# Three modulation tiles moved from the first gate group into the last attention steps

## The reference, cut to what matters

```python
c_act = jax.nn.silu(c)
for l in range(2):
    mod = c_act @ w_ada[l] + b_ada[l]                 # 6 * 1024 values
    sh_m, sc_m, gt_m, sh_f, sc_f, gt_f = jnp.split(mod, 6, axis=-1)
    h = rms_norm(x, g_mix[l]) * (1.0 + sc_m) + sh_m
    z = h @ w_in[l] + b_in[l]                         # qa ka va qi ki wi qb kb vb ga gb
    ...                                               # index scores, top 128, two attentions
    merged = sigmoid(ga) * y_a + sigmoid(gb) * y_b    # y_a = att_a @ w_oa, y_b = att_b @ w_ob
    x = x + gt_m * (merged @ w_out[l])
    h2 = rms_norm(x, g_ffn[l]) * (1.0 + sc_f) + sh_f
    x = x + gt_f * ((silu(gate) * up) @ w_down[l])    # gate, up = split(h2 @ w_gu[l])
```

## Time and profile before

| | us |
|---|---|
| median of 3 runs | 3172.62 |
| lowest, highest | 3166.37, 3175.24 |
| the profiled execution | 3175.28 |
| its span in the profile | 3173.7 |
| VectorE's first and last modulation tile of layer 0 in the attention steps | 289.39, 358.22 |

### The profile page before, as it was taken

How to read it: one execution, slowest core, us unless ns; L and a number is a source line. 1 busy time by engine, 2 the same in 40 slices (tenths; PEclk the granted TensorE clock), 3 DMA queues, 4 the chain that set the end, 5 groups by cost and what they waited for, 6 DMA issues and landing times.

```text
span 3173.7 us, 36875 instructions
## 1 busy us (share of the span) xinstructions
PE 3027.0 (95%) x14098; PEld 2309.5 (73%) x14098; DVE 1705.9 (54%) x2840; ACT 1258.9 (40%) x1912; POOL 1097.6 (35%) x538
## 2 busy tenths in 40 slices
PE   6999999999989999999998999999999998999998
PEld 4666777888856667788886777877777886666664
DVE  5687673222257868422213454655677137666664
ACT  4355434223245553422324444323334234455543
POOL 1242344444423324354442554444444441000001
PEclk9999999999999999999998999999999998999999
DMA  5122563443321137374332333524442335799995
GB/s 228 53 61 73 173 200 113 142 130 100 117 80 54 60 100 241 124 308 144 95 115 81 107 120 113 193 85 117 136 128 67 93 106 223 299 385 384 383 380 208
DMA packets 188508, 501.29 MB, mean 158 GB/s; under 512 B 20080, under 2 KB 98032, under 8 KB 172224
## 3 DMA queue, kind: packets, MB, share of 16 engines
q1 hardware_dynamic: 165808, 417.24, 38.9%
q0 software_dynamic: 13200, 49.32, 4.1%
q10 hardware_dynamic: 9344, 32.61, 3.0%
HBM read 463.83 MB, written 35.29 MB: 157 GB/s over the span
## 4 chain that ended last, share of the span: by engine, by line
PE 77%; DVE 12%; ACT 4%; DMA 3%; issue 2%; ACTq 1%; POOL 1%; DVEq 0%; SPq 0%; POOLq 0%
PE banks L741 18%; PE banks L743 18%; PE banks L742 18%; PE banks L1483 5%; PE banks L1464 3%; PE banks L1466 2%; PE banks L1465 2%; DMA ring<-in_w_all 2%; PE banks L856 1%; PE banks L877 1%; PE banks L733 1%; PE banks L866 1%; DVE abuf L2377 1%; ACT w_hi L1568 1%; PE banks L837 1%
## 5 line engine op out<-in xcount | busy, mean ns | idle before, releaser
L3063 POOL TENSOR_TENSOR w_lo<-ring,w_hi 128x1024 fp32r<-128x1024 f32 (+1 forms) x375 | 908.2, 2424 | 1377.0 <-ACT w_hi L1568 1376.8
L742 PE MATMUL banks<-h_lo,w_hi 128*128 128x512 f32 x2104 | 827.4, 393 | 0.0
L741 PE MATMUL banks<-hx_hi,w_hi 128*128 128x512 f32 (+2 forms) x1400 | 592.4, 423 | 20.2 <-POOL w_lo L3063 9.1
L1568 ACT ACTIVATE w_hi<-ring 128x1024 fp32r<-128x1024 f32 (+1 forms) x375 | 388.8, 1038 | 551.4 <-DMA ring<-in_w_all 482.5
L743 PE MATMUL banks<-hx_hi,w_lo 128*128 128x512 f32 (+2 forms) x1400 | 553.9, 396 | 0.0
L742 PEld LDWEIGHTS banks<-h_lo,w_hi 128*128 128x128 f32 x2104 | 399.3, 190 | 88.6 <-issue 11.0
L741 PEld LDWEIGHTS banks<-hx_hi,w_hi 128*128 128x128 f32 (+2 forms) x1400 | 266.7, 191 | 133.3 <-issue 62.4
L743 PEld LDWEIGHTS banks<-hx_hi,w_lo 128*128 128x128 f32 (+2 forms) x1400 | 266.0, 190 | 61.0
L741 PE MATMUL banks<-hf_hi,w_hi 128*128 128x512 f32 x704 | 274.8, 390 | 0.1
L743 PE MATMUL banks<-hf_hi,w_lo 128*128 128x512 f32 x704 | 274.0, 389 | 0.0
L2547 DVE TENSOR_TENSOR arena<-sgs,banks 128x512 f32<-128x512 f32 x44 | 30.3, 689 | 327.7 <-PE banks L743 327.7
(11 more groups left out here) (450 smaller groups left out, 5267.5 us busy)
## 6 DMA issues: line engine op xcount, KB each, us to landing
ring<-in_w_all SPq DMA_DIRECT2D x352, 512.0 KB, 3.9
arena<-in_w_all SPq DMA_DIRECT2D x26, 2048.0 KB, 13.9
arena<-in_w_all SPq DMA_DIRECT2D x100, 512.0 KB, 4.7
ring<-in_w_all SPq DMA_DIRECT2D x46, 1024.0 KB, 7.3
arena<-in_w_all SPq DMA_DIRECT2D x25, 1024.0 KB, 9.3
x<-in_w_all SPq DMA_DIRECT2D x23, 1024.0 KB, 9.6
abuf<-in_w_all SPq DMA_DIRECT2D x32, 512.0 KB, 5.5
routed<-abuf POOLq DMA_DIRECT2D x1, 12288.0 KB, 50.9
```

The costliest lines, as they stand in the source:

```text
L741: pe.matmul(bank[0:m, :], upper, hi, start=first, stop=False)
L742: pe.matmul(bank[0:m, :], upper, lo, start=False, stop=False)
L1568: act.activation(hi_at(u)[:, 0:n], raw_at(u)[:, 0:n], ACT.Copy).then_inc(w_upper, 1)
L3063: pool.tensor_tensor(lo_at(u)[:, 0:n], raw_at(u)[:, 0:n], hi_at(u)[:, 0:n], ALU.subtract)\
```

## The change

`EARLY` becomes 11. The attention steps that take a tile are now a list, `BESIDE_STEPS`: 17, 19, 21, 23, 25 as before, and then every step from 26 to 31, where before it was 27, 29 and 31. Gate group 0 takes none, the groups 1 to 7 three each as before. The places of the tiles behind the early ones are counted from the first of them, so that they start with place 0. SyncE's list follows: 11 tiles through place 3, and no tile loads in gate group 0. The second block has its own number (`EARLY2`) and is unchanged.

```diff
-EARLY, EARLY2 = 8, 16
+EARLY, EARLY2 = 11, 16
+BESIDE_STEPS = (17, 19, 21, 23, 25, 26, 27, 28, 29, 30, 31)
...
-            buf = (3 if self.turn < early else self.turn % 4) if n == 2 else 2 + self.turn % 2
+            buf = (3 if self.turn < early else (self.turn - early) % 4) if n == 2 else 2 + self.turn % 2
...
                 for t in range(8):
                     load()
-                    if t < 7:
+                    if 0 < t < 7:
                         load_tile()
                         load_tile()
                     load()
-                    if t < 6:
+                    if 0 < t < 6:
                         load_tile()
...
-                    if s >= 17 and s % 2:
-                        modulate_beside(16 + (s - 17) // 2, v1)
+                    if s in BESIDE_STEPS:
+                        modulate_beside(16 + BESIDE_STEPS.index(s), v1)
...
-                    for k in range(16 + EARLY + 3 * t, 19 + EARLY + 3 * t):
+                    for k in range(13 + EARLY + 3 * t, 16 + EARLY + 3 * t) if t else ():
                         modulate_beside(k, v1)
```

## The result

| | before | after |
|---|---|---|
| median, us (5 runs each, in turn) | 3171.7 | 3186.32 |
| lowest, highest | 3166.37, 3175.24 | 3185.66, 3191.63 |
| the profiled execution | 3175.28 | 3187.73 |
| its span | 3173.7 | 3186.2 |

The ratio is 1.0051, 95% interval [1.0039, 1.0062]: slower by 14.6 us between the medians, where 6.7 was forecast. Of the runs shown further down, one of the kernel before (3739.82 us) and one of `even_steps` (8937.16) lie far out; every ratio leaves them out, and the medians, which hold them, move by at most 0.4 us without them. The page of the profile says that TensorE's work did not grow; it waits more (before in the earlier trace rows).

What follows compares the result with a forecast made beforehand. The prediction took TensorE, busy 3027.0 of 3173.7 us, as the bound. Later `o_free` less unit 34's gain, 4.4 - 0.4 and 3.1 - 0.4, added 6.7 us to the median of 3172.62, giving 3179.3 us, range 3171 to 3187.

Steps and rivals of the forecast that it cites:

- The sign and the place: Slower by 6.7 us, from the end of the attention, with `o_free` 4.4 us later in layer 0, 3.1 in layer 1.
- group 0's tiles: Gate group 0: taking out three tiles, 3.84 us of VectorE per layer, gains nothing because VectorE waits for the sigmoid anyway.
- unit 34: Gate stage: the transfer of this weight unit, 6.53 us before, gets 0.4 us shorter in each layer.
- within 0.3%: Whole kernel: measured time within 0.3%, 9.5 us, of before; chance 0.73, against 0.24 slower and 0.03 faster.
- The turns of place 3: Attention steps 26 to 31: each tile waits a buffer turn, last lower half 4.4 us later in layer 0, 3.1 in layer 1.
- The collisions sort themselves out: Rival, gate group 1: GpSimd finishes before VectorE's tiles, winning back 3.7 us per layer, 3171.9 us; chance 0.22.
- A third collision: Rival, gate stage: another VectorE operation is caught by GpSimd's subtraction, 1.87 us more per layer, 3183.0 us; chance 0.20.
- The tail has room: Rival, attention's end: `o_free` does not move and the empty group 0 removes two gate gaps, 3167.2 us; chance 0.06.

Runs made afterwards that it cites:

- even_steps: The kernel before with its eight early tiles each one step earlier, in steps 16, 18 to 30: 3187.35 us, ratio 1.0044 to before.
- three_places: The changed kernel with the same steps, but early tiles from the sixth on going through places 0, 1 and 3: 3179.33 us, ratio 1.0026 to before.
- clear_of_gpsimd: Against `three_places`: eleven early tiles in odd steps only, one in step 29 and three in step 31: 3172.81 us, ratio 0.9999 to before.
- odd_double: Against `three_places`: two early tiles each in steps 27, 29 and 31, none in an even step from 26 on: 3179.71 us, ratio 1.0021 to before.

## Why the prediction was wrong

*The sign and the place* were right: slower, through the turns of place 3 and a later `o_free`; group 0's tiles bring nothing; no change worth its name between the last lower half and group 7 (1.0 us gained in the two layers together, 0.8 forecast for unit 34, whose transfer went from 6.53 to 5.86 us). The time, 3186.32, is just inside the range of 3171 to 3187, but the forecast was "within 0.3%" with 0.73, and it is slower by 0.51%.

*The step that failed* is "The turns of place 3": 4.4 and 3.1 us, where the tail measured 7.8 and 7.3. In it every tile was put at 1.28 us and the normalisation of step 31 at 0.88 us, though the earlier trace rows had shown 3.15 us for a tile beside GpSimd. I looked for that collision in gate group 1 only, and did not read GpSimd's row in the attention steps. The turns themselves were well sized. Taken from the tile of step 25, the start of step 31's was forecast at +32.2 us and came at +35.36. Of the 3.2 us between, 1.30 are the longer tile of step 26 and 0.87 that of step 28; 0.8 is the last transfer, which landed in 4.7 us and not 3.9. In layer 1 it is +34.98 against +31.2: 1.37 and 0.88 from the two tiles, and landings of 3.9 and 4.3 us where I used 3.3.

*A second path* was missed with it. The prediction had TensorE's last transposes 1.6 us later and took no cost from that. Counted from step 24's lower half they start after 31.53 us and not 25.35, so 6.2 later, and from there to the last values TensorE took 1.6 more at the half clock: together the whole 7.8. In layer 1 the two parts are 5.3 and 2.0 us of the 7.3. The added tiles and turns had pushed the mask of step 31 by 4.05 us, where 1.3 was forecast. VectorE, behind the last turn, had been free for only 0.3 us when these values came (0.54 in layer 1), so two arms end together. Removing the turns and keeping a tile in step 28 leaves 2.0 us per layer (`three_places`); removing that tile and the even steps altogether, with nothing pushed onto GpSimd ahead of TensorE, leaves nothing (`clear_of_gpsimd`). In the medians: about 7 us for all in place 3 (after to `three_places`), 6.6 for where the tiles stand in the steps (`three_places` to `clear_of_gpsimd`), 1.2, which is not told from nothing, for all else. The 7 us hold the normalisation's collision too, which three places took away with the turns: the two were not separated, as no kernel ran with place 3 alone and clear of GpSimd. Nor did one have a tile ahead of step 31's mask without a subtraction beside it; that 1.27 of 2.13 us there is the tile itself is arithmetic, not a run.

*The rivals.* "The collisions sort themselves out" did not happen: the tiles of group 1 are 3.42 and 3.31 us. "A third collision" had the right mechanism at the wrong place: 20.63 us to group 1's L2511 against 20.84 excludes it in the gate stage, and the attention has three in layer 0 and three in layer 1. The rule quoted with it, from the Trainium skill ("SBUF — State Buffer", "SBUF: two separate sides"), should have been applied to every step that a tile was moved into. The trace agrees there: the tiles of steps 26 and 28 took 2.58 and 2.15 us beside a subtraction. "The tail has room" was rightly given little for this change. With other steps and places the tail does have room; but its second half, that an empty group 0 then takes the gate gaps away, is wrong: they are 2.78 and 3.19 us in `clear_of_gpsimd`.

## What to carry to other kernels

Before work is moved to another step, read the timelines of both engines that share operands' memory at the new place, for the moved instruction and for everything that it pushes later: here an instruction that had cleared GpSimd by 0.4 us cost more than the work that pushed it. Count the turns of a buffer (use, signal, transfer) against the steps that ask for it; one more user of a single place added a full turn, of which 2.8 to 3.0 us reached the end of the attention, and with other places and steps the same tiles cost nothing that can be told. And when a chain of waits ends in a load, look at what the load stands behind in its issuing list: moving one line of that list gave 6.7 us, while no placing of the tiles went below the kernel before.

## What the runs showed of the hardware

- VectorE's normalisation, with one SBUF tensor and a per-partition scalar, took 2.58 to 2.83 us beside a GpSimd subtraction of 2.34 us, and 0.88 alone. A mask that reads PSUM and one SBUF tensor took 0.69 us beside a subtraction and alone. The modulation tile, with two SBUF inputs, took 2.14 to 3.42 us instead of 1.28. Where the tile started first it kept its 1.28 us and the subtraction took 2.99 (`clear_of_gpsimd`, 356.28 and 356.78). I had expected a collision of the tile only.
- TensorE's granted clock went from 1.00 to 0.50 after 3.72 us without work and a short run of transposes, and was back at 1.00 in the slice from 366; transposes of 1.06 us took 1.97. From the last transposes to the last values the fall cost 1.6 us (`odd_double`: 6.36 us against 4.75). With the gaps filled it stayed at 1.00, but the added matmuls ran longer than the gaps.
- In the kernel after, a lone tile landed in 3.5 to 3.7 us in layer 0 and in 3.1 to 3.9 in layer 1. With two others issued right behind it one took 4.7 and 4.3 us.
